# Local attention's weights as f16 halves, turned by one transposing DMA a slot, with values two slots behind the scores and the queries' halves made over all partitions

## The reference, cut to what matters

```python
def _swa_branch(q, k, v, g, sinks, cos, sin):
    q = _apply_rope(q.reshape(bsz, s, SWA_HEADS, HEAD_DIM), cos, sin)
    k = _apply_rope(k.reshape(bsz, s, SWA_KV_HEADS, HEAD_DIM), cos, sin)
    ...
    sc = jnp.einsum('bclkrd,bcmkd->bckrlm', qc, kw, preferred_element_type=f32) * (HEAD_DIM ** -0.5)
    sc = jnp.where(valid[None, :, None, None, None, :], sc, -jnp.inf)
    m = jnp.maximum(jnp.max(sc, axis=-1, keepdims=True), sink)
    p = jnp.exp(sc - m)
    p = p / (jnp.sum(p, axis=-1, keepdims=True) + jnp.exp(sink - m))
    o = jnp.einsum('bckrlm,bcmkd->bclkrd', p.astype(vw.dtype), vw).reshape(bsz, s, SWA_WIDTH)
    return o * jax.nn.silu(g)
```

## Time and profile before

| | us |
|---|---|
| median of 3 runs (1914.8 to 1917.05) | 1915.05 |
| the profiled execution | 1916.71 |
| its span | 1914.8 |
| PE busy / idle in the span | 1890.6 / 24.2 |
| DVE, ACT, POOL busy | 1172.4, 992.4, 393.5 |
| TensorE's granted clock | full speed in all 40 slices |
| mean busy share of the 16 DMA engines by the queue's packets | 39.3% |

### The profile page before, as it was taken

One profiled execution on the slowest core, in us unless ns is written; L12 is line 12 of the kernel. 1 busy time (PEld: TensorE's weight loads), 2 busy tenths in 40 slices (PEclk: granted clock), 3 DMA queues, 4 the chain that ended last, 5 costly groups with the idle time before them and its releaser, 6 DMA issues.

```text
span 1914.8 us, 27900 instructions
## 1 busy us (share of the span) xinstructions
PE 1890.6 (99%) x11048; PEld 1020.4 (53%) x11048; DVE 1172.4 (61%) x1555; ACT 992.4 (52%) x1912; POOL 393.5 (21%) x266
## 2 busy tenths in 40 slices
PE   7999999999999999999999999999999999999998
PEld 4446765455455664544454477554554555655443
DVE  6677556587436777654367765655873468776432
ACT  5674454465334666543356645544662356765421
POOL 0212021142222332111001130112332222321110
PEclk9999999999999999999999999999999999999999
DMA  6224334443334655434222252354333344554421
GB/s 191 88 88 150 104 106 138 121 122 90 109 105 131 155 128 165 112 132 146 59 67 88 72 166 89 106 150 120 110 105 110 113 137 126 148 138 116 165 84 44
DMA packets 264747, 224.68 MB, mean 117 GB/s; under 512 B 88400, under 2 KB 253226, under 8 KB 264618
## 3 DMA queue, kind: packets, MB, share of 16 engines
q1 hardware_dynamic: 264618, 222.90, 39.3%
HBM read 182.96 MB, written 2.16 MB: 97 GB/s over the span
## 4 chain that ended last, share of the span: by engine, by line
PE 87%; DVE 4%; ACT 3%; issue 2%; POOL 2%; DMA 1%; SPq 1%; DVEq 0%; ACTq 0%; POOLq 0%
PE PS L591 85%; POOL X L1694 1%; DVE Y L1338 1%; DMA X<-X 1%; PE PS L695 1%; DVE X L1338 1%; ACT Y L1077 1%; DVE wsp L1335 1%; SPq L512 1%; DMA stage<-w_in 1%; ACT Y L1078 0%; SPq L564 0%; POOL Y L1694 0%; PE PS L819 0%; ACT wsp L1000 0%
## 5 line engine op out<-in xcount | busy, mean ns | idle before, releaser
L591 PE MATMUL PS<-hT,wsp 128*128 128x512 f16 (+2 forms) x4968 | 1083.2, 377 | 1.0 <-ACT hT L981 1.0
L591 PEld LDWEIGHTS PS<-hT,wsp 128*128 128x128 f16 x4968 | 479.5, 98 | 562.8 <-issue 13.6
L1335 DVE SCALAR_TENSOR_TENSOR wsp<-stage,wsp 128x2048 f16<-128x2048 f32 x148 | 352.9, 2384 | 164.8 <-ACT wsp L1000 162.6
L591 PE MATMUL PS<-ys,wsp 128*128 128x512 f16 x1536 | 339.4, 379 | 0.0
L1000 ACT ACTIVATE wsp<-stage 128x2048 f16<-128x2048 f32 x148 | 281.3, 1901 | 46.6 <-PE PS L591 44.7
L591 PEld LDWEIGHTS PS<-ys,wsp 128*128 128x128 f16 x1536 | 149.4, 98 | 178.4 <-issue 4.1
L591 PE MATMUL PS<-wsp,hT 128*128 128x256 f16 x1728 | 193.2, 273 | 0.0
L591 PEld LDWEIGHTS PS<-wsp,hT 128*128 128x128 f16 x1728 | 168.6, 98 | 22.7 <-issue 2.3
L1003 ACT ACTIVATE X<-PS 128x512 f32<-128x512 f32 (+1 forms) x120 | 68.4, 593 | 140.5 <-PE PS L591 108.2
L1694 POOL TENSOR_TENSOR X<-X,K 128x1024 f32<-128x1024 f32 x26 | 62.7, 2412 | 351.3 <-DMA X<-X 351.3
L1694 POOL TENSOR_TENSOR M<-M,T 128x512 f32<-128x512 f32 x48 | 67.4, 1407 | 292.1 <-DVE T L1335 292.1
(11 more groups left out here) (195 smaller groups left out, 1974.4 us busy)
## 6 DMA issues: line engine op xcount, KB each, us to landing
stage<-w_in SPq DMA_DIRECT2D x120, 1024.0 KB, 5.0
stage<-w_branch SPq DMA_DIRECT2D x32, 1024.0 KB, 5.3
X<-X SPq DMA_DIRECT2D x120, 128.0 KB, 2.4
stage<-w_out SPq DMA_DIRECT2D x8, 1024.0 KB, 5.4
Y<-sums SPq DMA_DIRECT2D x8, 512.0 KB, 6.3
M<-sums SPq DMA_DIRECT2D x8, 512.0 KB, 5.9
Y<-Y SPq DMA_DIRECT2D x24, 128.0 KB, 3.2
xres<-x SPq DMA_DIRECT2D x4, 512.0 KB, 6.7
```

What stands on the lines that cost most here:

```text
L591: return pe.matmul(o, a, b, start=start, stop=stop, skip_group_check=True)
L1335: return dve.scalar_tensor_tensor(out=o, in0=a, scalar=c, in1=b, op0=op0, op1=op1)
```

## The change

Local attention's exponentials are still f32, but once they are normalised ScalarE makes their high f16 half (`local_hi`) and VectorE the low one (`local_lo`), both in `sH`, for both units of a slot together. One transposing DMA on SyncE's queue (`turn_local`) turns all 16 blocks of 128 x 128 of a slot to `sPT`, of which there are two. TensorE's f32 transposes and ScalarE's copy out of PSUM are gone. The values are multiplied two slots after the scores (before: one), as three f16 products; `vC` and `vE` are kept as f16 halves, so panel vc is now evacuated by ScalarE and VectorE. Maxima, sums, reciprocals and the normalising multiply are done once a slot for both units. VectorE's order in a local slot is new: the rotation's addition and `split_lo` stand ahead of the normalising multiply. The queries' high half is copied to `rhi` by ScalarE in one call over all partitions, the low half is made by VectorE in one call (it was GpSimd), and four DMAs (before: two) bring them to `qC`. The gates `gC` have three buffers. At a layer's start TensorE's `gates` wait for `dt_taken` (PSUM bank 4 read) in place of `dta_ready`.

```diff
@@ SyncE
+                def turn_local(k):
+
+                    sp.wait_ge(s["sw_hi"], at("sw_hi", k + 1, layer))
+                    sp.wait_ge(s["sw_lo"], at("sw_lo", k + 1, layer))
+                    if k >= 2:
+                        sp.wait_ge(s["sw_o"], at("sw_o", k - 1, layer))
+                    sp.dma_start_transpose(sPT[k % 2].rearrange("p h e (g n) -> p (h e g) n", n=P), sH.rearrange("p h e n -> p (h e n)"))\
+                        .then_inc(s["sw_turned"], 16)
...
+                            elif kind == "qc":
+                                moves = ((qC[i % 2][own, t], by_chunks(kind, rhi[own])), (qC[i % 2][other, t], by_chunks(kind, rlo[own])))
...
                     if DIFF0 <= p - 2 < DIFF0 + 16:
                         turn_differences(p - 2)
+                    if SWA0 <= p - 2 < SWA0 + 8:
+                        turn_local(p - 2 - SWA0)
@@ TensorE, before and local_out
-                    if SWA0 < p <= SWA0 + 8:
-                        for e in range(2):
-                            n = 2 * (p - 1 - SWA0) + e
-                            pe.wait_ge(s["sw_n"], at("sw_n", n + 1, layer))
-                            if n >= 2:
-                                pe.wait_ge(s["sw_y"], at("sw_y", n - 1, layer))
-                            for g in range(4):
-                                last = pe.transpose(PS[:, 5 + 2 * e, P * g:P * g + P], sE[:, e, g, :], ident)
-                            last.then_inc(s["sw_T"], 1)
...
-                    if SWA0 < p <= SWA0 + 8:
+                    if SWA0 + 2 <= p < SWA0 + 10:
...
-                                keys = (vC if c else vE)[:, i, HD * j:HD * j + HD]
-                                for t in range(2):
-                                    o = PS[HD * t:HD * t + HD, 5 + 2 * e, 0:PW].rearrange("p (u n) -> p u n", u=2)[:, :, HD * c:HD * c + HD]
-                                    last = mm(o, keys, sPT[:, e, 2 * c:2 * c + 2, HD * t:HD * t + HD], True, True)
+                                for k, (h, hp) in enumerate(((0, 0), (1, 0), (0, 1))):
+                                    keys = (vC if c else vE)[:, h, i, HD * j:HD * j + HD]
+                                    for t in range(2):
+                                        o = PS[HD * t:HD * t + HD, 6 + e, 0:PW].rearrange("p (u n) -> p u n", u=2)[:, :, HD * c:HD * c + HD]
+                                        exps = sPT[(n // 2) % 2][:, hp, e].rearrange("p (g n) -> p g n", n=P)[:, 2 * c:2 * c + 2, HD * t:HD * t + HD]
+                                        last = mm(o, keys, exps, k == 0, k == 2)
@@ TensorE, gates
-                                pe.wait_ge(s["dt_raw"], at("dt_raw", 1, layer))
-                                pe.wait_ge(s["dta_ready"], at("dta_ready", 1, layer))
+                                pe.wait_ge(s["dt_taken"], at("dt_taken", 1, layer))
@@ ScalarE
-                def local_turned(p):
...
-                            copy(sPT[:, e].rearrange("p g n -> p (g n)"), PS[:, 5 + 2 * e, :]).then_inc(s["sw_Ta"], 1)
+                def local_hi(p):
+                    if SWA0 <= p < SWA0 + 8:
+                        k = p - SWA0
+                        act.wait_ge(s["sw_n"], at("sw_n", k + 1, layer))
+                        if k >= 1:
+                            act.wait_ge(s["sw_turned"], at("sw_turned", 16 * k, layer))
+                        copy(sH[:, 0], sE.rearrange("p e g n -> p e (g n)")).then_inc(s["sw_hi"], 1)
...
-                        copy(dst[HD * t:HD * t + HD, t], by_chunks(kind, rcos[HD * t:HD * t + HD])).then_inc(s["rope_hi"], 1)
+                        copy(rhi, rcos).then_inc(s["rope_hi"], 2)
@@ VectorE
+                def rotated_lo(p):
...
+                        tt(rlo, rcos, rhi, ALU.subtract).then_inc(s["rope_lo"], 2)
+
+                def local_lo(p):
+                    if SWA0 <= p < SWA0 + 8:
+                        dve.wait_ge(s["sw_hi"], at("sw_hi", p - SWA0 + 1, layer))
+                        tt(sH[:, 1], sE.rearrange("p e g n -> p e (g n)"), sH[:, 0], ALU.subtract).then_inc(s["sw_lo"], 1)
...
                     scans(p)
+                    if SWA0 <= p < SWA0 + 8:
+                        rotated(p)
+                        for n in splits_in(p):
+                            split_lo(n)
                     before(p)
-                    if attention:
+                    if DIFF0 <= p < DIFF0 + 16:
                         rotated(p)
-                    local_gated(p)
-                    if attention:
                         for n in splits_in(p):
                             split_lo(n)
                     differences_lo(p)
+                    local_gated(p)
+                    local_lo(p)
                     evacuate(p, 0)
...
                     middle(p)
+                    rotated_lo(p)
                     if p > 0:
                         evacuate(p, 1)
```

More of the change, by code:

```diff
@@ L107 @@
 LOCAL_OUT_AT = 8
+LOCAL_SCORES = 2
 HEADS_AT = 6
@@ L543, in one_layer @@
                         sp.wait_ge(s["rope_lo"], at("rope_lo", 2 * rope_index(p - 4) + 2, layer))
+                        if kind == "qc" and i == 0:
+                            sp.wait_ge(s["ssd_out"], at("ssd_out", 8, layer))
+                        if kind == "qc" and i >= 2:
+                            sp.wait_ge(s["sw_s"], at("sw_s", 2 * (i - 1), layer))
                         for t, (own, other) in enumerate(((slice(0, HD), slice(HD, P)), (slice(HD, P), slice(0, HD)))):
@@ L704, in before @@
                                 pe.wait_ge(s["rope_stack"], at("rope_stack", stacked_after(1 + j), layer))
+                            if n >= 2 and e == 0:
+                                pe.wait_ge(s["sw_e"], at("sw_e", n // 2, layer))
                             own, prev, both = (slice(i * P, i * P + HD), slice(i * P - HD, i * P), slice(i * P, i * P + P))
@@ L1240, in after @@
                         falls(SSD_SLOT.index(p) + 1)
-                    if SWA0 < p <= SWA0 + 8:
-                        for e in range(2):
-                            n = 2 * (p - 1 - SWA0) + e
-                            j, i = divmod(n, 4)
-                            act.wait_ge(s["sw_y"], at("sw_y", n + 1, layer))
-                            if n == 0:
-                                act.wait_ge(s["tile_done"], at("tile_done", 2 * (SLOT[("br", 3)] + 1), layer))
-                            copy(Y_HI[0][:, 2 * j:2 * j + 2, i * P:i * P + P], sy[:, e]).then_inc(s["y_hi"], 1)
+                    if SWA0 + 2 <= p < SWA0 + 10:
+                        k = p - 2 - SWA0
+                        j, i = divmod(2 * k, 4)
+                        act.wait_ge(s["sw_y"], at("sw_y", k + 1, layer))
+                        if k == 0:
+                            act.wait_ge(s["tile_done"], at("tile_done", 2 * (SLOT[("br", 3)] + 1), layer))
+                        copy(Y_HI[0][:, 2 * j:2 * j + 2, i * P:i * P + PW], sy).then_inc(s["y_hi"], 1)
                     if PANELS[p][0] == "br" and PANELS[p][1] >= 12:
@@ L1480, in before @@
                     if SWA0 <= p < SWA0 + 8:
-                        for e in range(2):
-                            n = 2 * (p - SWA0) + e
-                            dve.wait_ge(s["sw_e"], at("sw_e", n + 1, layer))
-                            link(tt(srin[:, e], ssum[:, e], sd[:, e], ALU.add))
-                            link(dve.reciprocal(srin[:, e], srin[:, e]))
-                            tt(sE[:, e], sE[:, e], srin[:, e].unsqueeze(2).to_broadcast([P, 4, P]), ALU.mult)\
-                                .then_inc(s["sw_n"], 1)
+                        k = p - SWA0
+                        dve.wait_ge(s["sw_e"], at("sw_e", k + 1, layer))
+                        link(tt(srin, ssum, sd, ALU.add))
+                        link(dve.reciprocal(srin, srin))
+                        tt(sE, sE, srin.unsqueeze(3).to_broadcast([P, 2, 4, P]), ALU.mult).then_inc(s["sw_n"], 1)
                     if DIFF0 <= p < DIFF0 + 16:
```

194 lines of the change are left out of this document (100 added, 94 removed).

## The result

The changed kernel takes 1930.5 us (median of 4 runs, 1930.3 to 1933.4) against 1914.9 for the kernel before in the same session: ratio 1.0079, 95% interval 1.0067 to 1.0091. It is slower by 15.6 us, where 1909 was forecast; the time lies outside the range, on the side that had a chance of 0.10.

A forecast was written before the change was run, and what follows sets the result against it. TensorE, busy 99% of the span, was taken to bound the kernel: 1916.7 profiled, less 19.5 saved, plus 13.4 of new waits, gives 1910.6, by the median 1909 us. Range 1895 to 1918.

The forecast's parts named there:

- TensorE's terms: Savings on TensorE alone: transposes 13.9, values 3.2 and the second layer's start 2.4, together 19.5 us.
- Transposes: Local slots: TensorE's 128 transposes, 16 groups at 0.87 us, go; 13.9 us saved.
- Values: Local slots: 24 f16 matmuls with overlapping halves take 0.91 us for 1.11 a slot; 3.2 us saved.
- R3: Rival: the values' matmuls don't overlap, a local slot is 0.5 us longer, the kernel takes 1913; chance 0.16.
- Gates: Second layer's start: TensorE's wait for VectorE's last step before `dta_ready` goes; 2.4 us saved.
- The kernel without new waits: Rival: the local slots' two-slot dependence is hidden, TensorE gets no new waits, 1895.5 us; chance 0.17.
- The ring: Local slots: transposing DMA, swap, sines, `split_lo`, next low halves take 27.5 us against TensorE's 24.4; 11.8 us of waits.
- the cheap parts: Local stage: values' low half, `vE` copies and four query copies were each taken as hidden, costing TensorE nothing.
- over a slot of slack: Panel vc's slot: the values' low half on VectorE, 2 x 0.7 us, was taken as hidden.
- that cover: Third local slot: query copies land at 10.4 of the previous slot's 11.3 us, in time for its scores.
- the one at A3: TensorE's forecast wait of 2.8 us ahead of the fourth local slot's panel matmuls, in each layer.
- R2: Rival: swap held up behind the transposing DMA, 3.5 us more a trip, slower than before at 1923; chance 0.12.

The follow-up runs named there:

- e7: e3 with VectorE's low half of the first tile in the values' slot put behind the sum of the keys' rotation: 1906.1 us.
- e10: e7 with TensorE's first gates waiting for the decay's last step (`dta_ready`) again, as before the change: 1909.8 us.
- e8: e7 with GpSimd's low half of a differential query waiting for VectorE's two small subtractions of that slot: 1897.9 us.
- e5: Changed kernel with only the next pass's panel load issued ahead of a local slot's transposing DMA: 1921.6 us.
- e2: Changed kernel with the queries' halves made as before the change (low half by GpSimd, two DMA copies for four): 1935.3 us.
- e4: Changed kernel with a query panel's swap issued ahead of the same pass's transposing DMA: 1921.9 us.
- e3: Changed kernel with SyncE's transposing DMA of a local slot issued one pass later, ahead of the query copies: 1908.1 us.
- e11: Changed kernel with only GpSimd's low half of a differential query waiting for VectorE's two small subtractions of that slot: 1920.6 us.

## Why the prediction was wrong

**TensorE's terms were right.** Its busy time, which has no waits in it, went from 1890.6 us to 1873.1 in e7, where the clock is granted in full: 17.5 less, forecast 13.9 + 3.2 = 17.1. Transposes: gone. Values: (422.98 - 422.18) + 0.08 = 0.88 us a slot, forecast 0.91, so the halves overlap and R3 is out: 24 matmuls in 0.80 are 0.033 each, less than the 0.056 of a full f16 one. The prediction had set its bound without overlap, 1.42, beside what the Trainium skill's TensorEngine Tiling (Array Packing), Restrictions, says of the fast weight load; whether that was off here no row tells, but no such price shows. Gates: 2.4 by the earlier trace rows, gone in the changed kernel; e10 has them back. The kernel without new waits was put at 1895.5 by the median, and e8, which has 1.8 us of them left in its local slots, takes 1897.9.

**The ring was right, and hidden.** e5 shows it in place and nearly in size (2.69 and 2.40 in the first layer; e2: 2.94 and 3.51). The swap was issued right behind the transposing DMA as forecast, but 1.8 us into A2 and not 5 to 6, as A2 had started 3.55 late.

**The step that failed** is the one among the cheap parts: "the last copy is issued 2.0 later and lands 2.5 after that the earlier trace rows, at 10.4 of 11.3". TensorE could start on it only at 15.0. The copies' issue began 7.3 us into A1 where I had 5.9, and took 5.78 us where I had 2.7. I had taken the issue and the landing from rows in which nothing stood ahead of the copies, and did not follow past the transposing DMA what else it holds up: the panel load, which in the kernel before went 4.4 us ahead of the copies (400.89 and 405.33) and now moved its 1 MB just ahead of them (407.67 and 408.35). I named that cover and priced its loss at "part of the one at A3"; it was three waits a layer, 18.5 us in all, one of them at A6, where I had VectorE catching up. R2 had the right sign and half of the place (the swap behind the DMA, 8.6 us by e4), but its price was wrong: the transposing DMA's issue was 1.86 us in the median and not 3.81, its landing 4.3 and not 6.8.

**Terms that were missing.** The prediction had 13.4 us of waits, all from the ring; undoing the order of SyncE's queue gives 22.4 (e3). The waits for the copies fell there by 17.5 us (18.5 to 1.0), and the 4.7 us of the lower clock went with them, a cost that I had nowhere (6.0 in e5). The values' slot, "over a slot of slack": 2.0 by e7; slack for the low half's reader, but the instruction queued behind it had none. The meeting of VectorE and GpSimd in the differential attention: 8.2 (e8) to 10.0 (e11). I had weighed such meetings in the local slots alone. The kernel took 21.5 us over the forecast. The edits one on top of the other account for it: 22.4 - 13.4 = 9.0, 2.0 and 8.2, and 2.4 that e8 still lies above the time without waits, 21.6. But a chain of edits must close like this whatever its parts are, so the sum is no evidence of its own; each part rests on its own run and trace.

**Open.** Why GpSimd starts 0.06 us earlier, and whether the load stretches an issue by its descriptors or by its data; a smaller load in the same place was not tried.

## What to carry to other kernels

An in-order DMA queue is a list to be followed like an engine's: when something that waits is put into it, write down every transfer behind it, when that one used to go, and what it will land on top of. Here moving one call by one pass was worth 22 us, more than all that the change itself took from TensorE. And look at the instruction behind each new wait rather than at the reader of its result. A wait of 2 to 4 us on TensorE may bring a lower clock behind it, here 1.4 to 2.8 us more, which belongs in the range. A mean over a group can hide a mixture: 900 ns was two values, 417 and about 2350.

## What the runs showed of the hardware

- The issue of a DMA behind a 1 MB load on the same queue is stretched: four 128 KB copies 5.78 us for 2.87, a transposing DMA 5.16 for 2.77. With a transposing DMA right ahead and the load further ahead, the copies took 2.87, 3.13 and 4.51 in e5.
- After some waits of TensorE the granted clock fell to the 1.2 GHz level, and 24 panel matmuls took longer than 5.35 us: in e5 7.04, 6.90 and 8.14 after 2.69, 2.40 and 3.96; in e2 7.04 after 2.94 and 4.04, 8.16 after 3.44. After others it did not: 5.35 after 3.51 in e2, 5.34 after 3.55 and 2.88 in the changed kernel, which did lose after 3.25 and 2.54. The length of the wait alone does not tell.
- Of VectorE's two small subtractions the second was held up for 1.94 us when GpSimd started 0.12 or 0.13 us behind the first, and not when it started 0.18 us or more behind. The kernel before had 3 such meetings, the changed kernel 11; taking 6 or 7 away moved the kernel by 0.4 to 0.5%.
